# Second mixer's end: S5 gate and sums on GpSimd beside the retention, S5 output tiles ahead of the retention norm's rows

## The chip, the cores and the metric

One core of a Trainium2 chip runs the whole program in one launch. The metric is the device time of one execution in microseconds. The kernel has five compute engines' queues that matter here: TensorE (PE; PEld is its weight loads), VectorE (DVE), ScalarE (ACT), GpSimd (POOL), and SyncE (SP), which issues most of the transfers. Engines run their own instruction lists in order and meet only at semaphores.

## The reference

Two transformer blocks on 1024 tokens of width 1024. What matters here is the mixer of the second block: an S5 state-space branch and a retention branch, 512 channels each, concatenated and multiplied with an output matrix.

```python
y = jax.nn.gelu(y.reshape(bsz, seq_len, S5_WIDTH))
y_s5 = y * jax.nn.sigmoid(y @ glu_w + glu_b)            # end of s5_mixer
y_s5 = rms_norm_2(y_s5, s5_gain)                        # over all 512 channels of a token
...
out = intra + cross                                     # end of retention, 4 heads of 128
mu = jnp.mean(out, axis=-1, keepdims=True)
var = jnp.mean(jnp.square(out - mu), axis=-1, keepdims=True)
out = (out - mu) * lax.rsqrt(var + LN_EPS) * gn_gain
y_ret = out * jax.nn.silu(gate)
...
y = jnp.concatenate([y_s5, y_ret], axis=-1)
x = layer_norm(DEEPNORM_ALPHA * x + y @ w_out, ln1_g, ln1_b)
```

## The kernel before

Activations lie channels by tokens: a slot of `work` is 128 channels x 1024 tokens in f32, so the S5 branch has four slots (`TS`, gated in place by `UST`, squares in `YS`) and each retention head has one (`SCS[h]`). Products of large matrices are made in three parts: a rounded high part times a rounded high part (fp32r), and high times low (bf16) twice. So every operand of the output product needs a high part, written by ScalarE (a copy to `HR0`), and a low part, the difference, written by VectorE (`YSLO`, `YRLO`). Weights come the same way: SP loads a raw job (`load`), ScalarE makes its high part (`split_hi`), GpSimd its low part (`split_lo`, line 1805), in rings of three high, three low and two raw buffers. The output matrix is eight jobs, `pa0` to `pa3` for the S5 half and `pb0` to `pb3` for the retention half; each serves two output tiles of 128 channels.

PSUM is four buffers of 128x1024. A list `plan`, filled by `use(name, engine)`, gives each product its buffer (place modulo 4) and the engine that empties it; TensorE's `claim(name)` waits until the product four places earlier has been emptied, and `filled(engine, name)` waits for TensorE. So the order of that list is also an order of waits. The lists for the end of the second mixer stand at lines 261 to 270.

Order of the work there. TensorE (`mixer2_pe`): the four gate products `glu0` to `glu3`; the retention, eight steps for two pairs of heads (`kv`, `retained`), with VectorE updating the state between (line 2566) and ScalarE copying each half out (`roA`, `roB`); head sums `rm0` to `rm3` (`stats_matmuls`, line 411); token sums of the squares `rv0` to `rv3` and, for S5, `ss5` (`token_sums`, line 346: eight products of one column each); then rows, which bring a per-token root back across the partitions (`token_rows`, line 381): `rs5` for S5 and `rr0` to `rr3` for the heads; then the output tiles `p0a` to `p7a` (S5 half) and `p0b` to `p7b` (retention half) by `out_part`. VectorE (`mixer2_dve`): centering of the heads (2573), S5 gate (2577), sums of S5's squares (2580), the variances with their reciprocals (2584, 2586; 929 and 930 for S5), S5 norm (2595) each followed by a low part (2601), for each head the norm (2605), the gate (2607) and the low part (2610), then adding output tiles onto the input (2615 for the S5 half, 2618 for the other). ScalarE (`mixer2_act`; all its operations are recorded at line 2201): squares, roots, high parts, then the splits of the last five weight jobs. GpSimd (`mixer2_pool`) has nothing here until the split of `pa3`.

After the last output tile come the layer norm over 1024 channels and the feed-forward part of the second block.

## Time and profile before

| | us |
|---|---|
| median of 3 runs | 2593.65 |
| lowest, highest | 2591.98, 2594.05 |
| the profiled execution, its own time | 2592.05 |
| span of the profiled execution | 2590.2 |
| TensorE busy | 2438.2 (94%) |
| VectorE busy | 1432.1 (55%) |
| GpSimd busy | 931.0 (36%) |
| ScalarE busy | 920.6 (36%) |

The span runs from the first to the last instruction that the profile holds; the execution's own time is 1.85 us longer. Busy shares are means over the whole span, and the stages have different limits, so the rows below are of the stretch between 1640 and 1850 us. The chain of waits is followed back from the last instruction; a piece of it is what the end of the program waited for at that time.

### The profile page before, as it was taken

The page shows a single profiled execution, that of the slowest core. Times are in us where ns is not written, and L with a number is a line of the kernel's source. Part 1 is how long each engine was busy: PE and PEld are TensorE (multiplying, and loading weights), DVE is VectorE, ACT ScalarE, POOL GpSimd, SP SyncE. Part 2 cuts the span into 40 slices and gives each one's busy share as a digit, 9 for nine tenths or more (in the row PEclk, how much of TensorE's full clock was granted, in tenths as well). Part 3 has the DMA queues.
Part 4 walks back from the last instruction along what each step waited for, and adds up shares of the span by engine and source line. Part 5 has one row for each costly group of instructions (what it writes and reads, how often), then busy time and mean ns, then how long its engine had stood idle before and what let it go on. Part 6 is the DMA issues. An engine that isn't in the chain of part 4 may idle for free.

```text
span 2590.2 us, 37306 instructions
## 1 busy us (share of the span) xinstructions
PE 2438.2 (94%) x15140; PEld 1416.6 (55%) x15302; DVE 1432.1 (55%) x1604; ACT 920.6 (36%) x1241; POOL 931.0 (36%) x550
## 2 busy tenths in 40 slices
PE   4989989999899999999998999999789999999997
PEld 1655548885445555555554666575345555555553
DVE  5975656663596630566314875255587640466424
ACT  3245424440244520345213323221155431354314
POOL 0312121110255531555314888001336532455331
PEclk7999999999899999999998999989999999999998
DMA  8511020000301133111312622300122123211322
GB/s 332 227 58 49 14 110 3 3 3 16 122 25 49 60 105 120 64 51 50 123 67 111 114 61 79 122 1 25 51 80 66 49 89 108 89 52 63 121 79 76
DMA packets 55372, 200.00 MB, mean 77 GB/s; under 512 B 5793, under 2 KB 15521, under 8 KB 52257
## 3 DMA queue, kind: packets, MB, share of 16 engines
q1 hardware_dynamic: 47424, 180.05, 20.6%
q10 hardware_dynamic: 7776, 17.56, 2.0%
q8 instruction: 121, 1.98, 0.3%
q14 instruction: 51, 0.41, 0.1%
HBM read 168.22 MB, written 29.36 MB: 76 GB/s over the span
## 4 chain that ended last, share of the span: by engine, by line
PE 77%; DVE 11%; POOL 4%; issue 3%; DMA 3%; ACT 2%; SPq 0%; ACTq 0%; DVEq 0%; POOLq 0%; another core or an unknown queue 0%
PE pt L1306 16%; PE pt L1312 15%; PE pt L1309 15%; PE pt L1891 10%; PE pt L667 5%; PE pt L425 3%; PE pt L871 3%; PE pt L2768 2%; PE pt L2774 2%; PE pt L2771 2%; DMA work<-in_w_mod 1%; PE pt L346 1%; PE pt L411 1%; DVE work L621 1%; DVE work L3026 1%
## 5 line engine op out<-in xcount | busy, mean ns | idle before, releaser
L1256 POOL TENSOR_TENSOR slots<-work,weights_rounded 128x512 bf16<-128x512 f32 (+2 forms) x239 | 435.3, 1821 | 606.1 <-ACT weights_rounded L1428 317.6
L1309 PE MATMUL pt<-work,weights_rounded 128*128 128x512 bf16 x1208 | 327.8, 385 | 2.2
L1306 PE MATMUL pt<-rounded,weights_rounded 128*128 128x512 f32 x624 | 210.9, 455 | 12.6 <-POOL slots L1256 6.9
L1306 PE MATMUL pt<-rhs_rounded,weights_rounded 128*128 128x512 f32 x624 | 210.5, 454 | 7.2 <-DVE work L988 4.2
L1306 PE MATMUL pt<-hidden_rounded,weights_rounded 128*128 128x512 f32 x704 | 203.5, 424 | 0.3
L667 PE MATMUL pt<-work 64*64 64x64 f32 (+5 forms) x4668 | 187.6, 244 | 14.3 <-ACT work L553 6.9
L1309 PEld LDWEIGHTS pt<-work,weights_rounded 128*128 128x128 bf16 x1248 | 100.3, 99 | 169.4 <-issue 98.8
L667 PEld LDWEIGHTS pt<-work 64*64 64x64 f32 (+3 forms) x4668 | 160.5, 138 | 42.5 <-ACT work L553 11.2
L1312 PE MATMUL pt<-hidden_rounded,slots 128*128 128x512 bf16 x691 | 176.6, 387 | 1.1
L1422 ACT ACTIVATE weights_rounded<-work 128x512 fp32r<-128x512 f32 x196 | 123.8, 632 | 132.3 <-PE pt L1312 126.6
L1312 PE MATMUL pt<-rhs_rounded,slots 128*128 128x512 bf16 x607 | 168.9, 391 | 1.4 <-issue 0.2
L1312 PE MATMUL pt<-rounded,slots 128*128 128x512 bf16 x607 | 167.8, 389 | 1.4 <-issue 0.2
L1309 PE MATMUL pt<-slots,weights_rounded 128*128 128x512 bf16 x674 | 166.9, 381 | 1.3
L1428 ACT ACTIVATE weights_rounded<-work 128x1408 fp32r<-128x1408 f32 x37 | 51.1, 1381 | 292.7 <-PE pt L1312 292.4
L1306 PEld LDWEIGHTS pt<-hidden_rounded,weights_rounded 128*128 128x128 f32 x704 | 131.7, 188 | 41.6 <-POOL slots L1256 2.4
L1805 POOL TENSOR_TENSOR slots<-slots,weights_rounded 128x1024 bf16<-128x1024 f32 x28 | 66.7, 2383 | 238.5 <-ACT weights_rounded L2201 237.4
L1256 POOL TENSOR_TENSOR slots<-slots,weights_rounded 128x512 bf16<-128x512 f32 (+1 forms) x86 | 128.4, 1493 | 65.9 <-ACT weights_rounded L1422 63.5
L1306 PEld LDWEIGHTS pt<-rounded,weights_rounded 128*128 128x128 f32 x624 | 118.9, 191 | 56.2 <-issue 11.0
L1306 PEld LDWEIGHTS pt<-rhs_rounded,weights_rounded 128*128 128x128 f32 x624 | 118.3, 190 | 50.0 <-issue 5.5
L2742 POOL TENSOR_TENSOR slots<-slots,weights_rounded 128x1024 bf16<-128x1024 f32 x21 | 56.2, 2677 | 238.2 <-ACT weights_rounded L2897 237.9
L1575 DVE TENSOR_TENSOR slots<-pt,slots 128x512 f32<-128x512 f32 x120 | 83.0, 692 | 86.0 <-PE pt L1312 83.4
L1309 PEld LDWEIGHTS pt<-slots,weights_rounded 128*128 128x128 bf16 x704 | 63.9, 98 | 92.5 <-issue 31.0
(393 smaller groups left out, 4138.0 us busy)
## 6 DMA issues: line engine op xcount, KB each, us to landing
work<-in_w_up SPq DMA_DIRECT2D x64, 512.0 KB, 4.0
work<-in_w_down SPq DMA_DIRECT2D x37, 704.0 KB, 4.1
work<-in_w_mod SPq DMA_DIRECT2D x10, 2048.0 KB, 8.0
slots<-in_w_in SPq DMA_DIRECT2D x31, 512.0 KB, 3.6
slots<-in_w_up SPq DMA_DIRECT2D x24, 512.0 KB, 4.8
x_scratch<-work ACTq DMA_DIRECT2D x16, 512.0 KB, 2.6
work<-x_scratch SPq DMA_DIRECT2D x16, 512.0 KB, 7.8
slots<-in_w_v SPq DMA_DIRECT2D x10, 512.0 KB, 4.1
```

What stands on the lines that cost most here:

```text
L425: ins = pe.matmul(pt(name)[:, h * 512:h * 512 + 512], weights(k), w(s)[:, h * 512:h * 512 + 512], start=(k == 0), stop=(k == n - 1))
L667: return pe.matmul(out, lhs, rhs, start=start, stop=stop, skip_group_check=True)
L871: ins = pe.matmul(pt(f"o{m}")[:, h * 512:h * 512 + 512], w(WRAW + (NJOBS1 + m) % 2)[:, k * P:(k + 1) * P], w(s)[:, h * 512:h * 512 + 512], ...
L1256: did(pool, pool.tensor_tensor(dst, raw, high.bitcast(F32), ALU.subtract), name)
L1306: pe.matmul(out, whi[:, k * P:k * P + P], rhs_hi(k), start=first and k == ks[0], stop=False, skip_group_check=True)
L1309: pe.matmul(out, top_half(whi)[:, k * P:k * P + P], rhs_lo(k), start=False, stop=False, skip_group_check=True)
L1312: ins = pe.matmul(out, wlo[:, k * P:k * P + P], top_half(rhs_hi(k)), start=False, stop=last and k == ks[-1], skip_group_check=True)
L1422: did(act, act.activation(flat_hi(fast_block(half, j, p), 512), block_raw(half, j, BLOCKS[p]), ACT.Copy), "ffn_w_hi")
L1575: did(dve, dve.tensor_tensor(dst, src0, src1, ALU.add), "ffn_post")
L1805: G_(pool.tensor_tensor(p1_lo(n), p2_raw(n), p1_hi(n).bitcast(F32), ALU.subtract), "w_split")
L1891: return pe.matmul(o, l, r, start=start, stop=stop, skip_group_check=True)
L2742: did(pool, pool.tensor_tensor(p1_lo(n), p1_raw(n), p1_hi(n).bitcast(F32), ALU.subtract), "w_split")
```

## The change

The gate of S5 (`TS` times `UST`, four operations) and the three sums of its squares go from VectorE to GpSimd, right behind the gate products, with ScalarE's squares behind its four sigmoids. TensorE takes the S5 token sums `ss5` directly behind the retention, and the S5 row `rs5` directly behind the head sums, before the variances. VectorE does the S5 root ahead of the centering and the S5 norm right behind it. Two of the S5 low parts go to GpSimd, the other two stay on VectorE behind the first variance. The output tiles `p0a` to `p3a` go ahead of the rows `rr0` to `rr3`, with `p4a` to `p7a` behind them; VectorE's additions follow that order. ScalarE's splits of the jobs `pa3` and `pb0` go ahead of the retention's high parts. The list of PSUM places is changed to match. Context lines are left out of the diff.

```diff
--- before.py
+++ after.py
@@ -261,13 +261,12 @@
...
                         ("roA0", "act"), ("roA1", "act"), ("kv0", "dve"), ("kv1", "dve"), ("roB0", "act"), ("roB1", "act"),
-                        ("rm0", "dve"), ("rm1", "dve"), ("rm2", "dve"), ("rm3", "dve"), ("rv0", "dve"), ("rv1", "dve"),
-                        ("rv2", "dve"), ("ss5", "dve"), ("rv3", "dve"), ("rs5", "dve"), ("rr0", "dve"), ("rr1", "dve"),
-                        ("rr2", "dve"), ("rr3", "dve")]:
+                        ("ss5", "dve"), ("rm0", "dve"), ("rm1", "dve"), ("rm2", "dve"), ("rm3", "dve"), ("rs5", "dve"),
+                        ("rv0", "dve"), ("rv1", "dve"), ("rv2", "dve"), ("rv3", "dve")]:
             use(nm, eng)
-        for part in "ab":
-            for m in range(8):
-                use(f"p{m}{part}", "dve")
+        for nm in ([f"p{m}a" for m in range(4)] + [f"rr{h}" for h in range(4)] + [f"p{m}a" for m in range(4, 8)]
+                   + [f"p{m}b" for m in range(8)]):
+            use(nm, "dve")
         for t in (1, 2):
@@ -1847,6 +1846,10 @@
...
 
+            def s5_sum(m):
+                pool.wait_ge(E("s5_squares"), m + 1)
+                G_(pool.tensor_tensor(w(YS[0]), w(YS[0]), w(YS[m]), ALU.add), "s5_sums")
+
             split_lo(0)
@@ -1879,6 +1882,14 @@
...
                     outputs_through(it[1] + 1)
+            for m in range(4):
+                pool.wait_ge(E("pt_emptied_act"), ordinal[f"glu{m}"])
+                G_(pool.tensor_tensor(w(TS[m]), w(TS[m]), w(UST + m), ALU.mult), "s5_gated")
+                if m > 0:
+                    s5_sum(m)
+            for m in range(2):
+                pool.wait_ge(E("y_s5_hi"), m + 1)
+                pool.tensor_tensor(lo(YSLO, m), w(YS[m]), HR0[:, m, :].bitcast(F32), ALU.subtract).then_inc(E("y_s5_split"), 1)
             for n in range(job2["pa3"], NJOBS2):
@@ -2094,26 +2105,19 @@
...
                     retained(i, st)
+            ones = const("ones")[:, 0:1]
+            pe.wait_ge(E("s5_sums"), 3)
+            token_sums(pe, "ss5", w(YS[0]), ones, 1)
             pe.wait_ge(E("pt_emptied_act"), ordinal["roB1"])
...
                 stats_matmuls(pe, f"rm{h}", SCS[h], 1, const("ones"), None)
-            ones = const("ones")[:, 0:1]
-
-            def variance(h):
+            token_rows(pe, "rs5", ("rstd_sqrt", 4), one_row)
+            for h in range(4):
                 pe.wait_ge(E("ret_squares"), h + 1)
...
 
-            for h in range(3):
-                variance(h)
-            pe.wait_ge(E("s5_sums"), 3)
-            token_sums(pe, "ss5", w(YS[0]), ones, 1)
-            variance(3)
-            token_rows(pe, "rs5", ("rstd_sqrt", 4), one_row)
-            for h in range(4):
-                token_rows(pe, f"rr{h}", ("gn_sqrt", 3 + h + 1), lambda st, h=h: small(RVS + 8 * h + st).to_broadcast([P, P]))
-
-            def out_part(part, y_hi, y_lo, split):
-                for m in range(8):
+            def out_part(part, y_hi, y_lo, split, tiles=range(8)):
+                for m in tiles:
                     n = job2[f"p{part}{m // 2}"]
@@ -2123,8 +2127,8 @@
...
                         for k in range(4):
-                            if m == 0 and h == 0:
-                                pe.wait_ge(E(split), k + 1)
+                            if m == 0 and h == 0 and (part == "b" or k == 0):
+                                pe.wait_ge(E(split), k + 1 if part == "b" else 4)
                             mm(out, weights(n, at + k)[0], y_hi(k)[:, seq], k == 0, False)
@@ -2132,7 +2136,10 @@
...
 
-            out_part("a", lambda k: HR0[:, k, :], lambda k: lo(YSLO, k), "y_s5_split")
+            out_part("a", lambda k: HR0[:, k, :], lambda k: lo(YSLO, k), "y_s5_split", range(4))
+            for h in range(4):
+                token_rows(pe, f"rr{h}", ("gn_sqrt", 3 + h + 1), lambda st, h=h: small(RVS + 8 * h + st).to_broadcast([P, P]))
+            out_part("a", lambda k: HR0[:, k, :], lambda k: lo(YSLO, k), "y_s5_split", range(4, 8))
             out_part("b", lambda k: HR0[:, 4 + k, :], lambda k: lo(YRLO, k), "y_ret_split")
@@ -2291,6 +2298,9 @@
...
                 A_(w(TS[m]), pt(f"glu{m}")[:, :], ACT.Sigmoid, "pt_emptied_act", bias=col("s5_glu_b_2", m))
+            for m in range(4):
+                act.wait_ge(E("s5_gated"), m + 1)
+                A_(w(YS[m]), w(TS[m]), ACT.Square, "s5_squares")
             for i in range(2):
@@ -2301,17 +2311,10 @@
...
                        "pt_emptied_act" if hh else "act_step")
+            rstd_act(act, 4)
             for h in range(4):
...
                 A_(w(KZ[h]), w(SCS[h]), ACT.Square, "ret_squares")
-            for m in range(4):
-                act.wait_ge(E("s5_gated"), m + 1)
-                A_(w(YS[m]), w(TS[m]), ACT.Square, "s5_squares")
-            for h in range(4):
-                if h == 3:
-                    rstd_act(act, 4)
-                act.wait_ge(E("gn_recip"), 3 + h + 1)
-                A_(small(RVS + 8 * h, 8), small(RVS + 8 * h, 8), ACT.Sqrt, "gn_sqrt")
             for m in range(4):
@@ -2319,9 +2322,15 @@
...
             for h in range(4):
+                act.wait_ge(E("gn_recip"), 3 + h + 1)
+                A_(small(RVS + 8 * h, 8), small(RVS + 8 * h, 8), ACT.Sqrt, "gn_sqrt")
+            for n in range(job2["pa3"], job2["pb0"] + 1):
+                p2_done(act, n - 3)
+                split_hi(n)
+            for h in range(4):
                 act.wait_ge(E("y_ret"), h + 1)
                 A_(HR0[:, 4 + h, :], w(SCS[h]), ACT.Copy, "y_ret_hi")
-            for n in range(job2["pa3"], NJOBS2):
+            for n in range(job2["pb0"] + 1, NJOBS2):
                 p2_done(act, n - 3)
@@ -2568,16 +2577,21 @@
...
                            "pt_emptied_dve" if n == 14 and hh == 1 else f"state2_{i}")
+            rstd_dve(dve, "ss5", 1.0 / 512, LN_EPS)
             for h in range(4):
...
                    "pt_emptied_dve")
-            dve.wait_ge(E("pt_emptied_act"), ordinal["glu3"])
+            filled(dve, "rs5")
             for m in range(4):
-                V_(dve.tensor_tensor(w(TS[m]), w(TS[m]), w(UST + m), ALU.mult), "s5_gated")
-            for m in range(1, 4):
-                dve.wait_ge(E("s5_squares"), m + 1)
-                V_(dve.tensor_tensor(w(YS[0]), w(YS[0]), w(YS[m]), ALU.add), "s5_sums")
+                V_(dve.scalar_tensor_tensor(w(YS[m]).rearrange("p (n s) -> p s n", s=8),
+                                            w(TS[m]).rearrange("p (s n) -> p s n", s=8), col("s5_out_gain_2", m),
+                                            pt("rs5")[:, :].rearrange("p (s n) -> p s n", s=8), ALU.mult, ALU.mult),
+                   "y_s5" if m < 3 else "pt_emptied_dve")
+
+            def y_s5_low(m):
+                dve.wait_ge(E("y_s5_hi"), m + 1)
+                dve.tensor_tensor(lo(YSLO, m), w(YS[m]), HR0[:, m, :].bitcast(F32), ALU.subtract).then_inc(E("y_s5_split"), 1)
 
@@ -2585,20 +2599,19 @@
...
 
-            for h in range(3):
-                variance(h)
-            rstd_dve(dve, "ss5", 1.0 / 512, LN_EPS)
+            def x_a(m):
+                filled(dve, f"p{m}a")
+                dve.wait_ge(E(f"x_in{3 * (m // 4)}"), 32 if m >= 4 else 48)
+                V_(dve.scalar_tensor_tensor(w(H + m), w(H + m), ALPHA, pt(f"p{m}a")[:, :], ALU.mult, ALU.add), "pt_emptied_dve")
+
+            variance(0)
+            y_s5_low(2)
+            y_s5_low(3)
+            variance(1)
+            variance(2)
             variance(3)
-            filled(dve, "rs5")
-            for m in range(5):
-                if m < 4:
-                    V_(dve.scalar_tensor_tensor(w(YS[m]).rearrange("p (n s) -> p s n", s=8),
-                                                w(TS[m]).rearrange("p (s n) -> p s n", s=8), col("s5_out_gain_2", m),
-                                                pt("rs5")[:, :].rearrange("p (s n) -> p s n", s=8), ALU.mult, ALU.mult),
-                       "y_s5" if m < 3 else "pt_emptied_dve")
-                if m > 0:
-                    dve.wait_ge(E("y_s5_hi"), m)
-                    V_(dve.tensor_tensor(lo(YSLO, m - 1), w(YS[m - 1]), HR0[:, m - 1, :].bitcast(F32), ALU.subtract), "y_s5_split")
+            for m in range(4):
+                x_a(m)
             for h in range(5):
@@ -2609,10 +2622,8 @@
...
                        "y_ret_split")
-            for m in range(8):
-                filled(dve, f"p{m}a")
-                dve.wait_ge(E(f"x_in{3 * (m // 4)}"), 32 if m >= 4 else 48)
-                V_(dve.scalar_tensor_tensor(w(H + m), w(H + m), ALPHA, pt(f"p{m}a")[:, :], ALU.mult, ALU.add), "pt_emptied_dve")
+            for m in range(4, 8):
+                x_a(m)
             for m in range(8):
...
                 V_(dve.tensor_tensor(w(H + m), w(H + m), pt(f"p{m}b")[:, :], ALU.add), "pt_emptied_dve")
```

## Rows read from the trace of the kernel before

**Rows 1.** The page: the chain that ended last, shares of the span by engine.
```profile
PE 77%; DVE 11%; POOL 4%; issue 3%; DMA 3%; ACT 2%; SPq 0%; ACTq 0%; DVEq 0%; POOLq 0%; another core or an unknown queue 0%
```

**Rows 2.** Chain in order of time, 1700 to 1760: start us, us, what.
```profile
1710.95 0.61 ACT work L2201
...
1713.48 8.84 PE pt L411 x16
...
1723.67 1.24 DVE work L2577
...
1728.71 1.24 DVE work L2580
...
1732.51 6.99 PE pt L346 x32
1739.50 3.64 PE pt L381 x16
...
1756.67 1.29 DVE work L2605
...
1758.00 1.20 PE pt L1891 x4
```

**Rows 3.** Chain in order of time, 1640 to 1880, the last output tile.
```profile
1839.14 5.82 PE pt L1891 x25
```

**Rows 4.** GpSimd's groups, shapes apart: busy us, mean ns | idle before.
```profile
L1827 POOL TENSOR_TENSOR work<-work,slot 128x1024 f32<-128x1024 f32 x8 | 24.2, 3030 | 0.6
...
L1886 POOL TENSOR_TENSOR work<-work 128x1024 f32<-128x1024 f32 x3 | 7.1, 2370 | 37.7 <-ACT work L2201 37.4
```

**Rows 5.** Timeline of all engines, 1765 to 1830: start us, us, engine, line.
```profile
1771.83 2.38 POOL L1805 TENSOR_TENSOR slots<-slots,weights_rounded 128x1024 bf16<-128x1024 f32 x1 [123.58 <-ACT weights_rounded L2201]
1772.00 3.83 DVE L2615 SCALAR_TENSOR_TENSOR work<-work,pt 128x1024 f32<-128x1024 f32 x3
...
1813.74 2.38 POOL L1805 TENSOR_TENSOR slots<-slots,weights_rounded 128x1024 bf16<-128x1024 f32 x1 [8.46 <-ACT weights_rounded L2201]
1813.81 3.39 DVE L1017 TENSOR_TENSOR work<-work 128x1024 f32<-128x1024 f32 x1
```

**Rows 6.** ScalarE's timeline, 1640 to 1700.
```profile
1678.15 1.11 ACT L2201 ACTIVATE work<-pt,par 128x1024 f32<-128x1024 f32 x1 [5.75 <-PE pt L425]
1695.90 2.48 ACT L2201 ACTIVATE work<-pt 128x512 f32<-128x512 f32 x4 [16.63 <-PE pt L1891]
```

**Rows 7.** Groups by line, 1711 to 1758: busy us, mean ns | idle before.
```profile
L2201 ACT ACTIVATE work<-work 128x1024 f32<-128x1024 f32 x8 | 8.5, 1057 | 7.9 <-DVE work L2573 7.1 <-DVE work L2577 0.8
L2595 DVE SCALAR_TENSOR_TENSOR work<-work,par,pt 128x1024 f32<-128x1024 f32 x4 | 8.2, 2062 | 3.3 <-PE pt L381 3.2
...
L2201 ACT ACT_TABLE_LOAD x1 | 1.3, 1283 | 3.1 <-DVE small L2586 3.1
```

**Rows 8.** Single lines of VectorE: duration ns min/median/max, first and last start.
```profile
L2566 DVE SCALAR_TENSOR_TENSOR work<-work,cst,pt x60: 337/347/355, 1679.0 to 1707.8; 64x128 f32<-64x128 f32 x60
...
L2615 DVE SCALAR_TENSOR_TENSOR work<-work,pt x8: 1220/1222/1222, 1772.0 to 1801.7; 128x1024 f32<-128x1024 f32 x8
...
L1017 DVE TENSOR_TENSOR work<-work x9: 1224/1225/3393, 1813.8 to 2480.7; 128x1024 f32<-128x1024 f32 x9
```

**Rows 9.** Stretches: length, TensorE busy (count), granted clock, DMA share, GB/s.
```profile
1713.00:1717.00 4.00, 3.52 (x5) 0.57 0.00 0
...
1722.00:1727.00 5.00, 5.00 (x46) 1.00 0.01 2
1727.00:1732.00 5.00, 0.81 (x6) 0.52 0.00 0
1732.00:1739.00 7.00, 6.49 (x31) 0.50 0.00 0
...
1744.00:1749.00 5.00, 5.00 (x44) 0.98 0.01 3
```

**Rows 10.** TensorE's timeline, 1676 to 1762.
```profile
1722.14 5.66 PE L346 MATMUL pt<-cst,work 128*128 128x1 f32 x48
```

## The prediction

> **What bounds the kernel now.** I read the page's first lines, then the chain that ended last, then that chain in order of time through the end of the second mixer, then the engines' timelines there. TensorE holds 77% of the chain [rows 1], so time is won only where the chain leaves TensorE or where it runs work that need not be in line. The end of the second mixer is such a place. The last retention matmul ends at 1710.9, the first output tile (`p0a`) starts at 1758.00 [rows 2], and the sixteenth ends at 1844.97 [rows 3]. The reader is to see that the 47.1 us in between are one file of small steps: four copies by ScalarE, the head sums (L411), one centering, then seven VectorE operations that belong to S5 alone (L2577 four times, L2580 three times, 1723.67 to 1732.47), the token sums (L346), the S5 row (L381), VectorE's S5 norm, and only then output tiles. The 16 output tiles take 86.97 us, 5.44 each, at the full clock.
>
> **What goes, what is added, what moves.** I rebuild the chain from 1713.44, where the ScalarE copies end, and set it against before.
>
> *The gate and sums on GpSimd.* Seven operations leave VectorE: 8.8 us of the chain [rows 2]. On GpSimd an f32 operation of this size took 2.37 us at line 1886 and 3.03 on average at line 1827 [rows 4]; GpSimd stood idle for 123.6 us up to 1771.83 [rows 5]. ScalarE's last sigmoid ends at 1679.26 and its next work starts at 1695.90 [rows 6]. The squares stand behind all four sigmoids, so gates 0 and 1 are done early, squares 0 and 1 end at about 1681.5, and then GpSimd has five operations (sum 1, gate 2, sum 2, gate 3, sum 3) with squares 2 and 3 (1.06 us each [rows 7]) between: 5 x 2.45 + 2 x 1.2 gives 1696. At 3.03 each it is 1699. The sums are wanted at 1710.9, so this is hidden with 12 us to spare. Square 3 ends at 1693.3 (at 3.03 each: 1695.4), before ScalarE's copies are due. These five run beside VectorE's 60 state updates (L2566) [rows 8], which feed TensorE. I cost that at nothing: L2615, which like L2566 has one operand in SBUF and one in PSUM, ran three times from 1772.00 while GpSimd worked from 1771.83 to 1774.21 [rows 5], and none of its eight took over 1.222 us [rows 8]. Were it otherwise, see the second rival.
>
> *Token sums of S5 (`ss5`) first.* Eight products of one column (16 records in the trace) right after the retention, beside the four ScalarE copies (2.5 us [rows 2]). `ss5` and `rv3` took 6.99 us for both at the low clock of 1.2 GHz [rows 2, 9], so one is 3.5 us; at the full 2.4 GHz it is 1.9 (48 records in 5.66 us [rows 10]). The clock is still full there, so it hides. The root with its table load (1.28 us [rows 7]) is done at about 1715, while the head sums run.
>
> *Head sums*, unchanged: 8.84 us, 1713.48 to 1722.32. The first of them run at the low clock (0.57 granted over 1713 to 1717 [rows 9]), right after TensorE stood idle; I expect that to stay.
>
> *The S5 row (`rs5`)*: directly behind, with its root ready. 44 records of L381 in 5 us at a granted 0.98 [rows 9] give 1.8 us for 16, in place of 3.64 [rows 2]. End: 1724.2.
>
> *S5 norm*: VectorE, four strided operations of 2.06 us, 8.35 with their gaps [rows 7]. The four low parts no longer stand between them. End: 1732.6. The low parts 0 and 1 are GpSimd's (2.4 each, done by 1733), 2 and 3 are VectorE's: with ScalarE's last rounding (1.06) and one variance between, the last ends at about 1735.7.
>
> *`rv3`*: it takes the PSUM tile of `rs5`, so it waits for the fourth norm operation. By then TensorE has done `rv0` to `rv2`. In the trace 48 such records ran at the full clock until 1727, where it fell while they were still being issued (1.00, then 0.52), and 32 more ran entirely at 0.50 [rows 9, 10]. So `rv3` runs at half: 3.5 us, ending at 1736.1. That is the later of the two (low parts 1735.7), so output tiles start at 1736.1, 21.9 us before 1758.00.
>
> *Output tiles*: 86.97 us as before. *Rows of the retention norm* (`rr0` to `rr3`), which before lay under VectorE's S5 norm and in the gap before `p0a`: now four times 1.8, 7.3 us, on TensorE's path between `p3a` and `p4a`. *Clock*: `p0a` comes behind a row of low-clock products. Before, `rr3` stood ahead of it and took the low clock; now the tile itself does. The work that came behind idle time or one-column products stayed slow for 3.5 us in one place (the head sums, 1713.48 to 1717) and for 4.7 in another (L381, 1739.50 to about 1744.2) [rows 2, 9]. Half of it is lost: 1.7 to 2.4. I take 2.0, the middle.
>
> *What is moved past what.* Retention rows, their roots, gate multiplies and low parts: VectorE's work on them filled 1756.67 to 1772.00 [rows 2, 5], 15.3 us. It now starts when `rr0` is there and `x_a(3)` is through, about 1761, and ends near 1777. `p5a` to `p7a` claim PSUM tiles that `rr1` to `rr3` leave; `rr3` is left at about 1773 and wanted by `p7a` at about 1783. `p0b` wants all low parts and comes at 1789, so the cover is 12 us. Splits of weight jobs `pa3` and `pb0` go ahead of the retention's roundings in ScalarE's queue: they wait for `p1a` (1749) and `p3a` (1760), and nothing behind them is due earlier. GpSimd's split of `pa3` now comes behind the two low parts, 15 us before it is needed. SP's loads wait for those splits and come earlier with them, in the same order; SP's first load of the feed-forward weights stays tied to the last split, and moves with it.
>
> **Sum**, from 1713.48: 8.84 + 1.8 + 0.1 + 8.35 + 3.5 + 86.97 + 7.3 + 2.0 = 118.9, so `p7b` ends at 1832.4 against 1844.97. The gain is 12.5 us. Everything after it is a chain that starts from `p7b` and moves whole. The profiled execution took 2592.05 us (span 2590.2, 1.85 around it) and becomes 2579.6; the median of the runs shown is 1.6 above the profiled one. Forecast: 2581.2.
>
> **Rivals.**
> *First: the clock does not fall for the head sums.* With `ss5` in the 2.6 us gap, TensorE is never idle there. Of the 3.5 us at the low clock half would be saved, 1.75: gain 14.3, time 2579.4. For it: the low clock came right after an idle stretch. Against: single-column products did not keep the clock [rows 9]. The Trainium skill ("TensorE: Matmul & The Clock Gate", Part 1) ties the clock to how busy the engine is, and taken literally that speaks for this rival; the trace, where the engine counts as busy for all 5.00 us before the fall, speaks against it. Nothing else here hangs on the page.
>
> *Second, the other side: GpSimd holds up the retention.* Place: the 60 state updates between 1679.0 and 1707.8 [rows 8]. VectorE's L1017, both operands in SBUF, took 3.39 us in place of 1.22 when a GpSimd operation started just before it [rows 5, 8]: it stood until that was over. If the same held for L2566, five operations of 3.03 stop the state for 15.2 us, and ScalarE's squares, as late, hold its copies of the first half, which `roB0` claims, by another 3. Less 12.5: 5.7 us slower, 2599. It decides once the retention grows by more than 12.5. Against it: L2566 reads PSUM, like L2615; and its 60 instructions are 20.8 us of the 28.8 from 1679 to 1707.8, so that 8 us of a block could be made up. The Trainium skill ("GPSIMD Engine Reference", Key points) has contention only with two-port modes and two SBUF inputs, which would leave L2566 free; the pair L2615 and L1017 agrees.
>
> *Third: half of the gain comes back.* The late rows of the retention norm, or low parts 2 and 3 held by GpSimd (two SBUF operands each: up to 2 us apiece), or TensorE's reads slowed beside GpSimd, or `p4a` kept by VectorE's `x_a`. Together 5 to 9 us back: gain 4 to 8, near 2587. *Fourth: nothing moves*, because the low parts' four counts come later than I think and the file is merely reordered: 2593; it would need 20 us in the S5 norm that no row shows.
>
> **How the numbers follow.** Forecast 62%, first rival 17%, third 14%, fourth 3%, second 4%. The forecast's own width: `rv3` at full clock and `p0a` half as cold give 2.6 less (2578.5); a cold stretch of 4.7 and low parts 1 us late give 1.5 more, and the spread of the runs before is 2 us. The range goes from the first rival with the same width (2577) to the third (2588). About 0.2%, 5 us, is what a measurement of this kernel can tell from no change. Faster: forecast, first and most of the third, 0.90; same 0.06; slower 0.04.
>
> **What would show it.** Right: L346 records of `ss5` before the head sums; the first output tile at about 1736, 22 us before 1758; L381 in two places, 16 records behind the head sums and 64 after `p3a`; no idle TensorE between `p0a` and `p7b`; L2566 still at 0.347 us; half clock at the head sums and again at `p0a`. Wrong: L2566 or the retention (1679.3 to 1710.9) longer; TensorE waiting for VectorE at `p4a` or `p0b`; the sums on GpSimd ending after 1711; `p0a` later than 1740.

## The result and the profile after

| | before | changed |
|---|---|---|
| median, us | 2594.01 (6 runs) | 2580.68 (6 runs) |
| lowest to highest | 2591.98 to 2596.69 | 2579.34 to 2582.87 |
| profiled execution, its own time | 2592.05 | 2579.34 |
| its span | 2590.2 | 2577.4 |

The ratio is 0.9948, 95% interval 0.9935 to 0.9961: 13.3 us faster by the medians, where 12.5 were forecast; the median is 2580.68 for a forecast of 2581.2, and the profiled execution took 2579.34 for 2579.6. On the changed kernel's own page TensorE's share of the chain has gone from 77 to 78% and VectorE's from 11 to 10%.

The chain in order of time through the same stretch, changed kernel (start us, us, what; L345, L380, L410 and L1902 answer to L346, L381, L411 and L1891; L2587 is the S5 norm):

```profile
1681.10 32.75 PE pt L1902 x252
1713.85 1.88 PE pt L345 x16
1715.73 6.97 PE pt L410 x16
1722.70 1.80 PE pt L380 x16
...
1724.61 2.08 DVE work L2587
...
1733.21 3.54 PE pt L345 x16
1736.75 24.04 PE pt L1902 x96
1760.79 7.14 PE pt L380 x64
1767.94 65.03 PE pt L1902 x288
...
1833.06 1.23 DVE work L2629
```

Against [rows 2, 3]: the seven VectorE pieces (before: L2577, L2580) are gone, the S5 row stands right behind the head sums and takes 1.80 us instead of 3.64, the four pieces of the norm follow from 1724.61 without low parts between, and the first tile starts at 1736.75. The retention's first product is at 1681.10 here and was at 1679.3 before, so times in the stage have to be compared from its start. From there to VectorE's addition of the last tile (L2618 before at 1845.06, L2629 now at 1833.06) it is 151.96 us, before 165.74. Of these 13.8 us, 1.9 are the head sums (6.97 for 8.84), which x1 and x9 below show to be no effect of the change.

GpSimd's timeline, changed kernel (start us, us, engine, line, operation; L1887 gates, L1851 sums, L1892 low parts), then VectorE's state updates as one line (ns min/median/max), then TensorE's stretches (length, busy and count, granted clock, DMA share, GB/s):

```profile
1661.87 2.34 POOL L1887 TENSOR_TENSOR work<-work 128x1024 f32<-128x1024 f32 x1 [11.84 <-ACT work L2208]
...
1683.36 2.35 POOL L1851 TENSOR_TENSOR work<-work 128x1024 f32<-128x1024 f32 x1 [13.56 <-ACT work L2208]
...
1695.51 2.35 POOL L1851 TENSOR_TENSOR work<-work 128x1024 f32<-128x1024 f32 x1 [1.29 <-ACT work L2208]
1727.96 4.70 POOL L1892 TENSOR_TENSOR work<-work,rounded 128x1024 bf16<-128x1024 f32 x2 [30.11 <-ACT rounded L2208]
```

```profile
L2575 DVE SCALAR_TENSOR_TENSOR work<-work,cst,pt x60: 337/348/355, 1680.8 to 1709.6; 64x128 f32<-64x128 f32 x60
```

```profile
1713.00:1717.00 4.00, 4.00 (x31) 1.00 0.01 4
...
1727.00:1732.00 5.00, 4.44 (x25) 0.58 0.00 0
...
1737.00:1741.00 4.00, 4.00 (x10) 0.50 0.01 4
```

The third sum ends at 1697.9, 16 us before TensorE wants it; the 60 updates are as fast as in [rows 8]. The clock is full at the head sums, where it was 0.57 in [rows 9], falls while the variances are issued, and is low for the first tile.

### The profile page after: what moved, and what is told of

Read it like the earlier page. It is cut to its first block, busy times and chain, and to the rows that moved or that the text cites. A ratio compares the mean times of both kernels' runs of the same rounds, so it can differ in the third digit from the quotient of the medians.

```text
span 2577.4 us, 37467 instructions
## 1 busy us (share of the span) xinstructions
PE 2443.6 (95%) x15302; PEld 1412.5 (55%) x15302; DVE 1419.2 (55%) x1595; ACT 920.9 (36%) x1241; POOL 952.2 (37%) x559
## 4 chain that ended last, share of the span: by engine, by line
PE 78%; DVE 10%; POOL 3%; issue 3%; DMA 3%; ACT 2%; SPq 0%; ACTq 0%; DVEq 0%; POOLq 0%
PE pt L1305 16%; PE pt L1311 15%; PE pt L1308 15%; PE pt L1902 10%; PE pt L666 5%; PE pt L424 3%; PE pt L870 3%; PE pt L2779 2%; PE pt L2785 2%; PE pt L2782 2%; DMA work<-in_w_mod 1%; PE pt L345 1%; PE pt L380 1%; DVE work L620 1%; PE pt L410 1%
## 5 line engine op out<-in xcount | busy, mean ns | idle before, releaser
L1308 PE MATMUL pt<-work,weights_rounded 128*128 128x512 bf16 x1248 | 334.6, 386 | 0.0
L1308 PE MATMUL pt<-slots,weights_rounded 128*128 128x512 bf16 x704 | 172.6, 381 | 0.0
```

The source lines that it names most:

```text
L1308: pe.matmul(out, top_half(whi)[:, k * P:k * P + P], rhs_lo(k), start=False, stop=False, skip_group_check=True)
```

## The experiments

There were eleven runs, nine of new kernels and two of kernels run again (x9 is the changed kernel, x12 is x7), in three sets: x1 to x4, then x6 to x9, then x5, x11 and x12. Each set ran on one chip with its own runs of the kernel before (medians 2592.41, 2591.53 and 2592.04), and medians compare only within a set. The edits are shown in part; "..." stands for lines left out. A single execution scatters more than the differences sought: six runs of the changed kernel on the second chip went from 2574.5 to 2586.9, and six of x4 from 2574.1 to 2589.7. In the profiles most of that scatter lies outside the stage (the retention's first product comes anywhere from 1677.3 to 1686.8) and in the head sums. Each run has one profile, and that need not be a middling execution: x4's was the slowest of its six, x12's the slowest of its five, and those of the changed kernel, x3, x5, x6 and x8 the fastest of theirs. So beside the median I read the rest of the stage: from the end of the head sums (L410/L411) to VectorE's addition of the last tile.

| kernel | median, us | ratio (95%) | head sums, us | rest of the stage, us |
|---|---|---|---|---|
| before | - | - | 8.84 | 122.7 |
| changed | 2580.68 | 0.9948 (0.9935 to 0.9961) | 6.97 | 110.4 |
| x1, before with dead products | 2594.18 | 1.0009 (0.9998 to 1.0019) | 8.69 | 122.8 |
| x2, GpSimd part alone | 2588.55 | 0.9980 (0.9971 to 0.9990) | 8.64 | 114.9 |
| x3, order alone | 2598.89 | 1.0024 (1.0015 to 1.0033) | 7.15 | 127.2 |
| x4, rows first | 2580.46 | 0.9953 (0.9935 to 0.9971) | 10.05 | 110.9 |
| x9, changed again | 2581.05 | 0.9952 (0.9936 to 0.9968) | 8.67 | 110.8 |
| x6, wide dead products | 2584.87 | 0.9966 (0.9952 to 0.9979) | 8.61 | 112.3 |
| x7, high parts first | 2574.82 | 0.9933 (0.9918 to 0.9948) | 8.67 | 106.1 |
| x12, x7 again | 2577.53 | 0.9932 (0.9918 to 0.9947) | 8.44 | 107.7 |
| x8, low parts on VectorE | 2581.50 | 0.9957 (0.9943 to 0.9971) | 6.97 | 111.6 |
| x11, variances between | 2581.47 | 0.9952 (0.9938 to 0.9965) | 8.67 | 111.1 |
| x5, GpSimd longer | 2579.69 | 0.9948 (0.9931 to 0.9965) | 6.97 | 110.4 |

**x1: does `ss5` keep the clock?** The changed kernel's head sums ran at full clock with `ss5` in front, which is what the first rival had said. So the same kind of products was put into the kernel before.

```diff
+            claim(pe, "rm0")
+            for st in range(8):
+                pe.matmul(pt("rm0")[:, st:st + 1], w(KZ[0])[:, st * P:(st + 1) * P], const("ones")[:, 0:1], start=True,
+                          stop=True, skip_group_check=True)
             pe.wait_ge(E("pt_emptied_act"), ordinal["roB1"])
```

> The kernel before, with eight dead one-column products (16 records) put into TensorE's idle time between the retention and the head sums. Theory (one-column products keep the clock, as ss5 did in the changed kernel): the head sums take about 7.0 us in place of 8.84, at a granted 1.00, and may start 0.5 us later; the time is 1.4 to 1.9 us lower, near 2592.4. Rival (the head sums met a full clock by chance of phase, not through ss5): head sums 8.84 us with 0.57 granted in their first 4 us, time 2594.

Chain and stretches of x1, and the same stretches of x3, which has nothing in that gap:

```profile
1713.37 1.88 PE pt L2099 x16
1715.25 8.69 PE pt L411 x16
```

```profile
1713.00:1715.00 2.00, 2.00 (x24) 1.00 0.03 8
1715.00:1717.00 2.00, 2.00 (x6) 0.61 0.00 0
```

```profile
1711.00:1713.00 2.00, 1.53 (x4) 1.00 0.00 0
1713.00:1715.00 2.00, 2.00 (x6) 1.00 0.00 0
```

The dead products fill the gap (1713.37 to 1715.25) and the clock falls all the same as they end; the head sums take 8.69. In x3 TensorE stood idle for part of 1711 to 1713 and the head sums found a full clock. The median, 2594.18, is the one expected if `ss5` plays no part. Over the thirteen profiles, the head sums took 7.0 to 7.2 us in four and 8.4 to 10.1 in nine; with products in the gap in front it was three of eleven that kept the full clock, without them one of two. So products in the gap do not keep the clock, which was the rival's mechanism: the full clock in the changed kernel's profile was that execution's luck, and is not counted as gain.

**x2: the GpSimd part alone.**

```diff
-                        ("rm0", "dve"), ("rm1", "dve"), ("rm2", "dve"), ("rm3", "dve"), ("rv0", "dve"), ("rv1", "dve"),
-                        ("rv2", "dve"), ("ss5", "dve"), ("rv3", "dve"), ("rs5", "dve"), ("rr0", "dve"),
+                        ("ss5", "dve"), ("rm0", "dve"), ("rm1", "dve"), ("rm2", "dve"), ("rm3", "dve"), ("rv0", "dve"), ("rv1", "dve"),
+                        ("rv2", "dve"), ("rv3", "dve"), ("rs5", "dve"), ("rr0", "dve"),
...
+            for m in range(4):
+                pool.wait_ge(E("pt_emptied_act"), ordinal[f"glu{m}"])
+                G_(pool.tensor_tensor(w(TS[m]), w(TS[m]), w(UST + m), ALU.mult), "s5_gated")
+                if m > 0:
+                    s5_sum(m)
```

> The kernel before with only this part of the change: gate and sums on GpSimd, ScalarE's squares behind the sigmoids, ss5 directly behind the retention, its root ahead of the centering. The S5 row stays behind the variances, the low parts on VectorE between the norms, the retention norm's rows ahead of all output tiles. Theory (the gain is S5's vector work leaving the file): four variances 7.1 to 8 us, row 1.8 to 3.6, norm with low parts 13.4, first tile at about 67 us behind the retention's first product (before: 78.7), gain 10 to 12, about 2583. Rival (the gain is in the output tiles ahead of the rows): gain under 5, 2589 or more.

```profile
1716.73 8.64 PE pt L411 x16
1725.37 8.94 PE pt L346 x64
1734.31 3.26 PE pt L381 x16
...
1751.10 1.29 DVE work L2607
```

The rest of the stage is 7.9 us shorter than before, out of 12.4 in the changed kernel. That is less than expected: the first tile comes 70.35 us behind the retention's first product (1682.08), for about 67. The four variances took 8.94 us for 7.1 to 8 (the clock fell among them), the row 3.26, near the upper end of its 1.8 to 3.6, and VectorE's first retention norm (L2607) still stands ahead of the first tile at 1751.10, since `p0a` takes the PSUM tile of `rr0`, which that operation empties. The median gives only 3.9 us (2.6 to 7.5 by the interval), and 2588.55 lies next to the rival's 2589 and far from the theory's 2583. The rival's reason, the tiles ahead of the rows, is refuted by x4. In this profile the retention started 2.8 us later than before and what follows the stage took 1.6 us longer, and such amounts differ from profile to profile; but eleven executions should even them out, so why the median shows less than the stage stays open.

**x3: the order alone.**

```diff
-                        ("ss5", "dve"), ("rm0", "dve"), ("rm1", "dve"), ("rm2", "dve"), ("rm3", "dve"), ("rs5", "dve"),
-                        ("rv0", "dve"), ("rv1", "dve"), ("rv2", "dve"), ("rv3", "dve")]:
+                        ("rm0", "dve"), ("rm1", "dve"), ("rm2", "dve"), ("rm3", "dve"), ("rv0", "dve"), ("rv1", "dve"),
+                        ("rv2", "dve"), ("ss5", "dve"), ("rs5", "dve"), ("rv3", "dve")]:
...
+            for m in range(4):
+                V_(dve.tensor_tensor(w(TS[m]), w(TS[m]), w(UST + m), ALU.mult), "s5_gated")
+            for m in range(1, 4):
+                dve.wait_ge(E("s5_squares"), m + 1)
+                V_(dve.tensor_tensor(w(YS[0]), w(YS[0]), w(YS[m]), ALU.add), "s5_sums")
+            for h in range(3):
+                variance(h)
             rstd_dve(dve, "ss5", 1.0 / 512, LN_EPS)
```

> The changed kernel with S5's gate, sums and squares back on VectorE and ScalarE behind the centering, so that ss5, its root and rs5 come behind three variances; tiles p0a to p3a still ahead of the rows, low parts as in the changed kernel. Theory: first tile only 4 to 5 us earlier than before, and 7.1 us of rows and 2.3 us of low clock now on TensorE's path: 3 to 6 us slower than before, 2597 to 2600. Rival (the order is what gains): 2585 to 2589.

```profile
1711.46 7.15 PE pt L410 x16
...
1728.81 3.59 PE pt L345 x16
...
1734.62 3.77 PE pt L380 x16
...
1773.51 7.14 PE pt L380 x64
```

The median is 6.5 us above the kernel before, the rest of the stage 4.5 us longer, as the theory had it. `ss5` waits for VectorE until 1728.81, the row comes at 1734.62, and 7.14 us of rows (1773.51) now lie on TensorE's path, where before most of them lay under the S5 norm.

**x4: the retention norm's rows ahead of all tiles again.**

```diff
-        for nm in ([f"p{m}a" for m in range(4)] + [f"rr{h}" for h in range(4)] + [f"p{m}a" for m in range(4, 8)]
+        for nm in ([f"rr{h}" for h in range(4)] + [f"p{m}a" for m in range(8)]
...
-            out_part("a", lambda k: HR0[:, k, :], lambda k: lo(YSLO, k), "y_s5_split", range(4))
             for h in range(4):
                 token_rows(pe, f"rr{h}", ("gn_sqrt", 3 + h + 1), lambda st, h=h: small(RVS + 8 * h + st).to_broadcast([P, P]))
-            out_part("a", lambda k: HR0[:, k, :], lambda k: lo(YSLO, k), "y_s5_split", range(4, 8))
+            out_part("a", lambda k: HR0[:, k, :], lambda k: lo(YSLO, k), "y_s5_split")
```

> The changed kernel with the four rows of the retention norm, and VectorE's and ScalarE's work on them, ahead of all output tiles again. Theory: TensorE's sum is the same (rows 7.1 us, tiles 87), only that the rows wait 0.7 us longer for the last root and take the low clock: within 1.5 us of the changed kernel, 2580 to 2582.5. Rival (tiles ahead of the rows hide VectorE's 15 us): 7 us or more slower than the changed kernel, 2588.

```profile
1719.54 2.18 PE pt L345 x16
1721.72 10.05 PE pt L410 x16
...
1742.25 3.54 PE pt L345 x16
1745.80 10.11 PE pt L380 x64
1755.91 0.93 PE pt L1902 x4
```

The edit also puts VectorE's additions of `p0a` to `p3a` and ScalarE's splits of `pa3` and `pb0` back behind the retention norm. The time is that of the changed kernel (0.9953 and 0.9948), and the rest of the stage has 0.5 us more. The interval (0.9935 to 0.9971) leaves room for a few microseconds either way, but not for the rival's 2588. The rows took 10.11 us here instead of 7.14, since they and not the tile met the low clock, and the tiles ran at full clock. So the tiles' place ahead of the rows, half of the change's title, is worth nothing that can be measured: either way TensorE is the bound from `rv3` on, and VectorE's 15 us on the retention norm lie under output tiles.

**x9: the changed kernel again, x8: its low parts.**

> The changed kernel once more, as the mark for the runs beside it and as a second look at the clock. Theory (the clock at the head sums is a matter of phase, since the dead products of x1 and ss5 in x2 and x4 did not keep it): the head sums are anything from 7.0 to 10 us, and the stage from the retention's first product to p7b's end is 152 to 156 us; median 0.4 to 0.6% under the kernel before. Rival (ss5 keeps it): 7.0 us again.

```profile
1714.88 8.67 PE pt L410 x16
...
1737.57 24.50 PE pt L1902 x96
```

The same kernel has head sums of 8.67 us here, not 7.0, so it was the execution and not the edit that decided; and the ratio stays at 0.9952. In x8 the two low parts went from GpSimd back to VectorE:

```diff
-            for m in range(2):
-                pool.wait_ge(E("y_s5_hi"), m + 1)
-                pool.tensor_tensor(lo(YSLO, m), w(YS[m]), HR0[:, m, :].bitcast(F32), ALU.subtract).then_inc(E("y_s5_split"), 1)
...
-            y_s5_low(2)
-            y_s5_low(3)
+            for m in range(4):
+                y_s5_low(m)
```

> The changed kernel with all four S5 low parts on VectorE behind the first variance. Theory: VectorE's last low part comes 2.4 us later, at the time where rv3 plus 1.6 us stands; first tile 1.6 us later, and the time 1.6 us higher. Rival (GpSimd's low parts slow VectorE's norm as much as they help): no change.

```profile
1714.06 6.97 PE pt L410 x16
...
1731.86 4.63 DVE work L2591 x4
...
1736.63 23.73 PE pt L1899 x96
```

The chain now runs through four low parts of VectorE (4.63 us). The first tile comes 57.20 us behind the retention's first product (1679.43), against 55.65 in the changed kernel, 1.55 later as expected. The rest of the stage is 1.2 us longer, and the medians (2581.50 and 2581.05 in x9) are 0.45 us apart, which is not distinct from none: the price of 1.6 us shows in the chain and not in the time.

**x5: GpSimd beside the retention for longer.**

```diff
+            for _ in range(5):
+                G_(pool.tensor_tensor(w(TMP), w(TMP), w(TMP), ALU.subtract))
```

> The changed kernel with five more dead GpSimd operations (f32, 128x1024) behind the third sum, so that GpSimd works through the second half of the retention as well, up to about 12 us after the third sum. Theory (VectorE's state updates read one operand from PSUM and are not held up): updates at 0.347 us in the median and 0.36 at most, retention 32.75 us, time as the changed kernel. Rival (GpSimd holds them up a little, unseen in five operations): retention longer by over 0.5 us, updates over 0.4 us.

GpSimd's timeline and VectorE's updates in x5:

```profile
1694.89 9.77 POOL L1891 TENSOR_TENSOR slot<-slot 128x1024 f32<-128x1024 f32 x5
```

```profile
L2577 DVE SCALAR_TENSOR_TENSOR work<-work,cst,pt x60: 337/347/356, 1677.8 to 1706.5; 64x128 f32<-64x128 f32 x60
```

GpSimd worked without a break from 1694.89 to 1704.66 (9.8 us, less than the 12 I had reckoned with), inside the updates' 1677.8 to 1706.5, and their median is 347 ns and the longest 356. The retention took 32.75 us, as in every kernel here, and the time is the changed kernel's (0.9948). VectorE's updates are not held up.

**x6, x7, x12, x11: what is still in the gap.** In the changed kernel `rv3` waits for the norm because it takes the PSUM tile of `rs5`, the low parts are ready at 1735.90, 0.85 us before the first tile, and `p0a` runs at 1.2 GHz. x6 tries to hold the clock with wide dead products:

```diff
+            def keep_busy(name, n):
+                for _ in range(n):
+                    mm(pt(name)[:, 512:1024], top_half(p1_hi(wide))[:, 0:P], top_half(p1_hi(wide))[:, 0:512])
...
                 token_sums(pe, f"rv{h}", w(KZ[h]), ones, 1)
+                keep_busy(f"rv{h}", (4, 4, 10, 4)[h])
```

> The changed kernel with 22 dead bf16 products of 512 columns among the four variances (4, 4, 10, 4), about 4.7 us of work that fits the time TensorE stands idle or slow there. Theory (one-column products leave the clock to fall, wide ones hold it): granted 1.00 from rs5 to p0a, rv3 1.8 in place of 3.54 us, p0a to p3a 21.8 in place of 24.0; first tile at about 0.8 us earlier; 3 us under the changed kernel. Rival (idle time alone decides, and 1.8 us of it remain either way): clock falls as before, and the filler makes the variances later: 0 to 3 us slower.

```profile
1728.00:1730.00 2.00, 2.00 (x15) 0.61 0.00 0
...
1732.00:1734.00 2.00, 2.00 (x11) 0.50 0.00 0
...
1736.00:1738.00 2.00, 2.00 (x6) 0.50 0.00 0
```

The clock fell nevertheless, at about 1728.4 (worked out from the 0.61 over 1728 to 1730), the filler then ran at the low clock too, and the rest of the stage grew by 1.5 to 1.9 us against x9 and the changed kernel. The clock was back before `p0a`, which therefore ran fast, but later. The median is 3.8 us above x9's, beyond the 0 to 3 of the rival, and the rival's reason does not hold either: TensorE was busy without a break when the clock fell (2.00 of 2.00 us).

x7 takes the waits away instead:

```diff
-                        ("rv0", "dve"), ("rv1", "dve"), ("rv2", "dve"), ("rv3", "dve")]:
+                        ("rv", "dve")]:
-        for nm in ([f"p{m}a" for m in range(4)] + [f"rr{h}" for h in range(4)] + [f"p{m}a" for m in range(4, 8)]
+        for nm in ([f"p{m}a" for m in range(4)] + ["rv3"] + [f"rr{h}" for h in range(4)] + [f"p{m}a" for m in range(4, 8)]
...
+            for k in range(4):
+                pe.wait_ge(E("y_s5_hi"), k + 1)
+                for seq in halves:
+                    mm(pt("p0a")[:, seq], weights(n, k)[0], HR0[:, k, :][:, seq], k == 0, False)
+                for seq in halves:
+                    mm(pt("p0a")[:, seq], weights(n, k)[1], top_half(HR0[:, k, :][:, seq]), False, False)
+            pe.wait_ge(E("y_s5_split"), 4)
+            for k in range(4):
+                for seq in halves:
+                    ins = mm(pt("p0a")[:, seq], top_half(weights(n, k)[0]), lo(YSLO, k)[:, seq], False, k == 3)
+            ins.then_inc(E("pt_filled"), 1)
+            out_part("a", lambda k: HR0[:, k, :], lambda k: lo(YSLO, k), "y_s5_split", range(1, 4))
+            pe.wait_ge(E("ret_squares"), 4)
+            token_sums(pe, "rv3", w(KZ[3]), ones, 1)
```

> The changed kernel with the variances of heads 0 to 2 in one PSUM tile, that of head 3 behind p3a, and p0a's products ordered so that those that need only high parts go first, each as its high part comes. Theory (rv3 waits for the S5 norm only because it takes rs5's tile, 0.85 us beyond the low parts, and p0a waits for low parts it needs last): p0a ends 4 us earlier, head 3's variance costs 1.8 behind p3a: 2 us under the changed kernel. Rival (the low clock takes it back, since p0a now starts in a colder stretch): within 1 us of it.

> The kernel of x7 once more, as the mark for x11 beside it. Theory: 5 to 7 us under the changed kernel's 2581, so 2574 to 2576, 0.6 to 0.7% under the kernel before. Rival (x7's median was luck of its six runs; by its chain it should gain only 2 to 4): 2577 to 2579.

VectorE and ScalarE treat the variances of three heads as one block of 24 columns, behind the low parts. Chain of x7 (L1902 at 1726.31 is the variances of three heads and the tiles `p0a` to `p3a`, L345 at 1756.58 the fourth variance, L380 the rows):

```profile
1724.53 1.78 PE pt L380 x16
1726.31 30.27 PE pt L1902 x144
1756.58 1.68 PE pt L345 x16
1758.25 7.25 PE pt L380 x64
1765.51 65.03 PE pt L1902 x288
```

The same piece in x12:

```profile
1731.48 31.86 PE pt L1902 x144
```

From the row's end the chain no longer leaves TensorE. The rest of the stage is 106.1 and 107.7 us in the two profiles, 2.7 to 4.3 under the changed kernel's 110.4; x12 has less because the low clock reached further into `p0a` (31.86 us for 30.27). The time is 0.9933 and 0.9932 of the kernel before, in two sets, against 0.9948, 0.9952 for the changed kernel. It is faster than the kernel before, and 6.2 us faster than the changed one in the medians of one set, though their intervals against the kernel before overlap (0.9918 to 0.9948, and 0.9936 to 0.9968). The repeat does not confirm that size: its median, 2577.53, is where the rival had it (2577 to 2579), 2.2 us under x5, which is as fast as the changed kernel, while its ratio is as good as x7's. The 3 to 4 us that the chains show are what can be relied on. Of all kernels here it has the lowest median in its set both times.

> The kernel of x7 with the variances of heads 0 to 2 standing one each ahead of p0a's products of high part 0, 1 and 2, so that they fill the 1 us waits between those. Theory: variances 3 x 1.8, high parts 4 x 1.03 and low parts 1.75 end at about 11.5 us behind rs5 if the clock stays full, against 14 in x7: 2.5 us under x7. Rival (the clock falls in that stretch all the same, as it did in x6 with wide products among the variances): under 1 us.

x11 moved the three variances between the high parts' products. TensorE's timeline (`cst` marks variances, `rounded` the products):

```profile
1727.48 1.84 PE L1902 MATMUL pt<-cst,work 128*128 128x1 f32 x16
1731.03 1.22 PE L1902 MATMUL pt<-rounded,weights_rounded 128*128 128x512 f32 x2 [1.71 <-ACT rounded L2232]
...
1732.93 3.41 PE L1902 MATMUL pt<-cst,work 128*128 128x1 f32 x16
...
1738.07 3.41 PE L1902 MATMUL pt<-cst,work 128*128 128x1 f32 x16
```

After the first variance TensorE waits 1.7 us for the first high part, and from 1731 on the clock is low; variances 2 and 3 take 3.41 us each in place of 1.84. The rest of the stage is 111.1, all of x7's gain given back, and the median is 3.9 us above x12's in the same set, where 2.5 us below x7 were expected and under 1 us by the rival. The rival's reason, that the clock falls all the same, was the right one. The order in x7, which does most of the variances before the clock falls (all 48 records in 6.71 us, in x12 7.50), is the better one.

## Why the prediction was right

Step by step, with its own terms, from the end of ScalarE's copies (1715.21 in the changed kernel) to the end of the last tile at 1832.96: 117.75 us, forecast 118.9.

- *GpSimd hides gate and sums.* Right. Operations took 2.35 us, square 3 was over at 1695.4 and the third sum at 1697.9, which in the kernel before's time is 1696.1, as forecast (1696). What it is worth is shown by x3 against the changed kernel: 16.8 us in the rest of the stage when the same work goes back to VectorE. Of these 8.8 are the operations; the last centering (1.3), `ss5` (3.6) and its root with the table load (2.2) come onto the chain with them, the row takes 3.77 us for 1.80 at the low clock, and 1.1 are saved between the norm and the first tile.
- *`ss5` hides beside the copies.* Nearly: the copies ended at 1715.21, the head sums began at 1715.73, when `ss5` was through. That is 0.5 us that the sum did not hold, and it goes back to a misreading. The prediction took 1710.9 for the end of the retention and so had a gap of 2.6 us for `ss5`; 1710.9 is only where the chain turns to ScalarE. TensorE's timeline of the kernel before has the retention running to 1712.07 and a gap of 1.41 us, into which the 1.88 us of `ss5` do not fit:

```profile
1679.32 32.75 PE L1891 MATMUL pt<-work 128*128 128x256 f32 x252 [0.40 <-ACT work L2201]
1713.48 8.83 PE L411 MATMUL pt<-work,cst 128*128 128x512 f32 x16 [1.41 <-ACT work L2201]
```

- *Head sums unchanged.* In the profile they took 6.97, not 8.84, and x1 and x9 show that this says nothing of the change. This is the term that was furthest off, by 1.9 us; at 8.84 this stage would have come out 0.7 us over the forecast.
- *The S5 row* 1.80 us for 1.8. *The norm* 8.46 for 8.35.
- *`rv3` at half clock, waiting for the tile of `rs5`*: 3.54 for 3.5. The low parts were ready 0.85 us before it ended, forecast 0.4. x7, which took this wait away together with that for the low parts, gained.
- *Rows on TensorE's path* 7.14 for 7.3. *Low clock at the first tile*: `p0a` to `p3a` took 24.04 us where four tiles at full clock take 21.7, a loss of 2.3 for 2.0 (in x9 24.50, a loss of 2.8).
- *Cover for what was moved.* Right: TensorE did not wait from `p0a` to `p7b`, and VectorE was through with the retention norm at 1778.3 (its last line below), 11.3 us before `p0b`, which comes four tiles (4 x 5.42) behind 1767.94, at 1789.6; forecast were 12.

```profile
1775.79 2.48 DVE L2623 TENSOR_TENSOR work<-work,rounded 128x1024 bf16<-128x1024 f32 x2
```

The mechanism is thus the one that was forecast. That the median came within 0.5 us of the forecast is in part luck: single executions of the changed kernel lie up to 12 us apart (2574.5 to 2586.9 in x9), and in the profile the stage from 1713.44 was 13.8 us shorter, of which 1.9 were the fast head sums, so that 11.9 stand against the 12.5. One sign that was named for being right, the half clock at the head sums, is missing from the changed kernel's profile and is there in x9's (granted 0.50 from 1716 to 1719).

Of the rivals, the first gave about the same time (2579.4) by a mechanism that x1 refutes, with x2, x4 and x9, where `ss5` stood in the gap and the head sums were slow. The second, GpSimd holding up the retention, is refuted by the changed kernel's updates and by x5. What it was built on is still there: in the changed kernel too, VectorE's L1016, both operands in SBUF, took 3.39 us from 1801.81, beside a GpSimd operation from 1801.73. The third and fourth did not come.

What the prediction left open and the experiments settled is where the gain sits. It is not in putting tiles ahead of rows (x4 against the changed kernel: 0.5 us), and not in the order as such (x3: 6.5 us slower). It needs both that S5's vector work runs beside the retention (x2 alone: 7.9 us of the rest of the stage) and that the S5 row then goes ahead of the variances and the low parts out of the norm, since only then the first tile's inputs are ready early (another 4.5; x4 against x2 gives 4.0 for this part without the tiles' new place). How the gain divides between the two is less sure than that both are needed: by the ratios x2 has about 5 us and x4 about 12.

## What to carry to other kernels

At a joint between two stages, list which engine's work there depends on nothing late, and give it to an engine that idles through the stage before; an order change alone gains nothing while the first input of the new order is still late. After such a change look at which operand the first product of the next stage needs last: here products that need only high parts could start while the low parts were made, which was worth another few microseconds. And do not read a change of TensorE's clock in one profile as an effect of the edit before the same edit has been tried on the other kernel.

## What the hardware showed that I had not expected

The granted clock at the same place differs from one execution to the next, although TensorE did the same before it: head sums of 6.97 us in one profile of the changed kernel and 8.67 in the next (x9), 10.05 in x4. Neither eight one-column products in an idle gap (x1) nor 22 wide bf16 products among 64 one-column records (x6) kept it at 2.4 GHz. The Trainium skill ("TensorE: Matmul & The Clock Gate", Part 1) says of the rise to the full clock after a kernel's start that it comes at a point which varies from run to run. No reading here is of a start; of a change in the middle of a kernel the changed kernel and x9 show the same, with 1.7 us between them.
